# Turning the residual stream's tiles by VectorE blocks and DMA instead of TensorE transposes, in a two-layer decoder trunk

## What is computed

```python
def reference(x, p, g_mix, g_ffn, g_ple, g_final, ...):
    h = x
    for i in range(DEPTH):
        xn = rmsnorm(h, g_mix[i])
        if i % 2 == 0:
            mix = attn_mixer(xn, i, w_in_attn[j], ..., w_out_attn[j])
        else:
            mix = rglru_mixer(xn, w_in_rec[j], ..., w_out_rec[j])
        h = h + mix
        h = h + swiglu(rmsnorm(h, g_ffn[i]), w_ffn_gate[i], w_ffn_up[i], w_ffn_down[i])
        gate = jax.nn.sigmoid(rmsnorm(h, g_ple[i]) @ w_ple_gate[i])
        h = h + gate * (p[i] @ w_ple_proj[i])
    return rmsnorm(h, g_final)
```

## Time and profile before

| | us |
|---|---|
| median of 3 runs | 2414.16 (2414.1 to 2416.4) |
| the profiled execution | 2416.15 |
| its span | 2414.4 |
| VectorE busy | 1333.5 (55%) |
| ScalarE busy | 1128.5 (47%) |
| hardware DMA queue q1, share of 16 engines | 60.2% |
| granted TensorE clock | 0.997 of full |

### The profile page before, as it was taken

One profiled execution on the slowest core, in us unless ns is written; L12 is line 12 of the kernel. 1 busy time (PEld: TensorE's weight loads), 2 busy tenths in 40 slices (PEclk: granted clock), 3 DMA queues, 4 the chain that ended last, 5 costly groups with the idle time before them and its releaser, 6 DMA issues.

```text
span 2414.4 us, 29406 instructions
## 1 busy us (share of the span) xinstructions
PE 2387.1 (99%) x10908; PEld 1974.2 (82%) x10908; DVE 1333.5 (55%) x1655; ACT 1128.5 (47%) x1467; POOL 3.2 (0%) x17
## 2 busy tenths in 40 slices
PE   8999999999999999999999999999999999999997
PEld 7888778888888888888888888888888888888886
DVE  5545666555554555444466677554555555544455
ACT  5425545544444444444454575454444434444454
POOL 0000000000000000000000000000000000000000
PEclk9999999999999999999999999999999999999999
DMA  7744445666766666655557455566766667655563
GB/s 219 235 119 120 123 137 174 182 202 183 226 203 197 216 189 210 202 191 191 191 186 237 146 163 169 191 187 194 218 196 205 212 183 230 201 191 192 191 207 134
DMA packets 250938, 455.42 MB, mean 189 GB/s; under 512 B 21816, under 2 KB 38240, under 8 KB 250720
## 3 DMA queue, kind: packets, MB, share of 16 engines
q1 hardware_dynamic: 250800, 454.18, 60.2%
q10 hardware_dynamic: 48, 0.02, 0.0%
HBM read 440.49 MB, written 2.10 MB: 183 GB/s over the span
## 4 chain that ended last, share of the span: by engine, by line
PE 96%; DVE 1%; ACT 1%; DMA 1%; SPq 0%; issue 0%; ACTq 0%; DVEq 0%
PE ps L1338 30%; PE ps L1340 30%; PE ps L1339 30%; PE ps L1292 1%; PE ps L1549 1%; PE ps L1462 1%; DMA raw<-in_w_in_rec_dram 1%; PE ps L1393 1%; ACT w_hi L571 0%; PE ps L1474 0%; DVE w_lo L816 0%; SPq L494 0%; PE ps L1499 0%; ACT junk L627 0%; PE ps L1500 0%
## 5 line engine op out<-in xcount | busy, mean ns | idle before, releaser
L816 DVE TENSOR_TENSOR w_lo<-raw,w_hi 128x1024 fp32r<-128x1024 f32 x820 | 996.0, 1220 | 996.5 <-ACT w_hi L571 992.4
L571 ACT ACTIVATE w_hi<-raw 128x1024 fp32r<-128x1024 f32 x820 | 859.5, 1054 | 1092.0 <-PE ps L1340 925.1
L1338 PE MATMUL ps<-w_hi,xa_hi 128*128 128x512 f32 x1664 | 647.9, 389 | 0.0
L1340 PE MATMUL ps<-w_hi,xa_lo 128*128 128x512 f32 x1664 | 647.4, 389 | 0.0
L1339 PE MATMUL ps<-w_lo,xa_hi 128*128 128x512 f32 x1664 | 647.3, 389 | 0.0
L1340 PEld LDWEIGHTS ps<-w_hi,xa_lo 128*128 128x128 f32 x1664 | 312.3, 188 | 65.1
L1339 PEld LDWEIGHTS ps<-w_lo,xa_hi 128*128 128x128 f32 x1664 | 312.3, 188 | 64.7
L1338 PEld LDWEIGHTS ps<-w_hi,xa_hi 128*128 128x128 f32 x1664 | 312.3, 188 | 64.4
L1338 PE MATMUL ps<-w_hi,xb_hi 128*128 128x512 f32 x864 | 349.0, 404 | 3.9 <-DVE xb_lo L879 2.3
L1340 PE MATMUL ps<-w_hi,xb_lo 128*128 128x512 f32 x864 | 338.1, 391 | 0.0
L1339 PE MATMUL ps<-w_lo,xb_hi 128*128 128x512 f32 x864 | 337.3, 390 | 0.0
(11 more groups left out here) (201 smaller groups left out, 1022.0 us busy)
## 6 DMA issues: line engine op xcount, KB each, us to landing
raw<-in_w_ffn_gate_dram SPq DMA_DIRECT2D x176, 512.0 KB, 4.5
raw<-in_w_ffn_up_dram SPq DMA_DIRECT2D x176, 512.0 KB, 4.5
raw<-in_w_ffn_down_dram SPq DMA_DIRECT2D x176, 512.0 KB, 4.1
raw<-in_w_in_attn_dram SPq DMA_DIRECT2D x88, 512.0 KB, 3.6
raw<-in_w_ple_gate_dram SPq DMA_DIRECT2D x64, 512.0 KB, 4.3
raw<-in_w_in_rec_dram SPq DMA_DIRECT2D x64, 512.0 KB, 4.1
raw<-in_w_out_attn_dram SPq DMA_DIRECT2D x32, 512.0 KB, 4.3
raw<-in_w_out_rec_dram SPq DMA_DIRECT2D x32, 512.0 KB, 4.0
```

The costliest lines, as they stand in the source:

```text
L571: nc.scalar.activation(w_hi[:, s, 0:n], raw[:, s, 0:n], ACT.Copy).then_inc(hi_ready, 1)
L816: nc.vector.tensor_tensor(w_lo[:, s, 0:n], raw[:, s, 0:n], w_hi[:, s, 0:n].bitcast(F32), ALU.subtract).then_inc(lo_ready, 1)
L1338: nc.tensor.matmul(o, xh[:, k, tok], w_hi[:, s, wk], start=(k == 0), stop=False)
L1340: ins = nc.tensor.matmul(o, xl[:, k, tok], w_hi[:, s, wk], start=False, stop=(k == nkt - 1))
```

## The change

`Kind` gets a flag `move`. It is set for resid, for up, and for ple in layer 0; those kinds have no PSUM banks to turn any more. One path then serves them all:

- VectorE, behind `evacuate` at slot 3: two block transposes, from `stage` for up and from h for the others, into `sg`.
- SyncE: 16 DMAs from `sg` to `stage`, behind the load of slot 7 of the chunk that follows the turned one. Each writes two runs of 128 elements per partition where it wrote one of 256.
- ScalarE, behind the split of slot 6: waits for the 16 DMAs, rounds (one instruction for up, four with a gain for the others).
- VectorE, behind the split of slot 6: the remainders (one or four instructions).
- TensorE: the transposes of h for resid and ple chunks go. In a phase's first chunk it waits for `tiles_ready` instead of `turn_used`.
- ScalarE's sigmoid in ple, which writes `sg`, waits for the moves before it; so does the first gate chunk of an FFN.

```diff
-    resid = Kind("resid", "v", 2, True)
+    resid = Kind("resid", "v", move=True)
...
-        ph.append(Phase(f"ffn{layer}", 11, (8, 8), (Kind("gate", "a"), Kind("up", "v")), "A",
+        ph.append(Phase(f"ffn{layer}", 11, (8, 8), (Kind("gate", "a"), Kind("up", "v", move=True)), "A",
...
-        ple = Kind("ple", "v", 0 if last else 2, True)
+        ple = Kind("ple", "v", move=not last)
...
+            def move_blocks(q, i, r):
+
+                if not q.kinds[r].move:
+                    return
+                sp.wait_ge(blocks_turned, move_no(q, i, r))
                 for a in range(4):
                     for c in range(4):
-                        sp.dma_start(st_blocks[32 * c:32 * c + 32, a], sg_blocks[32 * a:32 * a + 32, c]
-                                     ).then_inc(hid_moved, 16)
+                        sp.dma_start(st_blocks[32 * c:32 * c + 32, :, a],
+                                     sg_blocks[32 * a:32 * a + 32, c].rearrange("p (m x) -> p m x", m=NT)
+                                     ).then_inc(blocks_moved, 16)
...
-                    if (c := hid_chunk(q, i, r, j, 1)) is not None:
-                        move_hid(*c)
+                    if j == 8:
+                        move_blocks(*prev)
+                    if j == 0 and prev and prev[0].slots[prev[2]] == 8 and (two := two_before(q, i, r)):
+                        move_blocks(*two)
                     load_slot(q, i, r, j)
...
+            def round_tiles(q, i, r):
+
+                if not q.kinds[r].move:
+                    return
+                c = column(q, i, r)
+                hi = X[q.dst][0]
+                act.wait_ge(blocks_moved, move_no(q, i, r) * 256)
+                if q.gain is None:
+                    ins = nc.scalar.activation(by_blocks(hi, c), moved_all, ACT.Copy)
+                else:
+                    for k in range(4):
+                        ins = nc.scalar.activation(tile_by_blocks(hi, 4 * c + k), moved_tile(k), ACT.Copy,
+                                                   scale=gain_ap(q.gain, 4 * c + k))
+                ins.then_inc(tiles_hi, 1)
...
                     split_slot(q, i, r, j)
-                    if (c := hid_chunk(q, i, r, j, 1)) is not None:
-                        round_hid(*c)
+                    if j == 6:
+                        round_tiles(*prev)
...
+            def turn_blocks(q, i, r):
+
+                k = q.kinds[r]
+                if not k.move:
+                    return
+                dve.wait_ge(evac["v"], evac_no(q, i, r)[1])
+                c = column(q, i, r)
                 for m in range(NT):
+                    rows = stage[:, m] if k.name == "up" else h[:, m, c * CW:(c + 1) * CW]
+                    dst = sg_blocks.rearrange("p c (m k t) -> p m c k t", k=4, m=NT)[:, m]
+                    ins = nc.vector.transpose(dst, rows.rearrange("p (k c d) -> p c k d", k=4, c=4))
+                ins.then_inc(blocks_turned, 1)
...
                     if j == 3:
                         evacuate(*prev)
-                    if prev[0].kinds[prev[2]].name == "up" and j == 4:
-                        turn_hid(prev[0], prev[1])
-                    if (c := hid_chunk(q, i, r, j, 2)) is not None:
-                        split_hid(*c)
+                        turn_blocks(*prev)
+                    if j == 6:
+                        split_tiles(*prev)
...
-                    elif q.src == "H":
-                        pe.wait_ge(hid_ready, hid_no(q.before, (2 * j + 1) // 4))
+                    elif q.before and q.before.per_move:
+                        pe.wait_ge(tiles_ready, move_no(*maker(q.before, (2 * j + 1) // 4)))
                     else:
                         pe.wait_ge(turn_used, src_turn0(q) + bank_of_ktile(q, j) + 1)
...
-                elif k.name in ("resid", "ple"):
-                    c = 2 * i + r
-                    transpose4(lambda m, f: h[:, m, c * CW + f * P:c * CW + (f + 1) * P], t0)
```

More of the change, by code:

```diff
@@ L64, with __init__ @@
 class Kind:
-    def __init__(self, name, evac, banks=0, split=False):
+    def __init__(self, name, evac, banks=0, split=False, move=False):
         self.name, self.evac, self.banks, self.split = name, evac, banks, split
+        self.move = move
 class Phase:
@@ L123, in build_phases @@
                         stat=6 if last else 3))
-    slot, va, turn, hi = 0, {"v": 0, "a": 0}, 8, 8
+    slot, va, turn, hi, move = 0, {"v": 0, "a": 0}, 8, 8, 0
     for p in ph:
@@ L133, in build_phases @@
         p.per_hi = sum(k.banks for k in p.kinds if k.split)
+        p.move0, p.per_move = move, sum(k.move for k in p.kinds)
+        move += p.per_move * p.pairs
         p.per_v = {e: sum(k.evac == e for k in p.kinds) for e in "va"}
@@ L168, in hi_no, with move_no, maker @@
     return i * p.per_hi + (p.hi0 + sum(k.banks for k in p.kinds[:r] if k.split))
+def move_no(p, i, r):
+    return i * p.per_move + (p.move0 + sum(k.move for k in p.kinds[:r + 1]))
+def maker(p, c):
+    return (p, c, 1) if p.loop else (p, *divmod(c, 2))
 def two_before(p, i, r):
@@ L342, in trunk @@
         turned, turn_hi, turn_used = sem("turned"), sem("turn_hi"), sem("turn_used")
-        hid_turned, hid_rounded, hid_ready = sem("hid_turned"), sem("hid_rounded"), sem("hid_ready")
-        hid_moved = sem("hid_moved")
+        blocks_turned, blocks_moved = sem("blocks_turned"), sem("blocks_moved")
+        tiles_hi, tiles_ready = sem("tiles_hi"), sem("tiles_ready")
         consts, ident_ready, gmix_in = sem("consts"), sem("ident_ready"), sem("gmix_in")
@@ L421, in trunk, with moved_tile, by_blocks, tile_by_blocks @@
         sg_blocks = sg[:].rearrange("p m c -> p (m c)").rearrange("p (c x) -> p c x", c=4)
[L422 to L440, removed]
+        st_blocks = stage[:].rearrange("p m (a x) -> p m a x", a=4)
+        moved_all = st_blocks.rearrange("p m a (k t) -> p (m a) k t", k=4)
+        def moved_tile(k):
+            return moved_all[:, :, k]
+        def by_blocks(t, c):
+            tiles = slice(4 * c, 4 * c + 4) if isinstance(c, int) else bass.ds(4 * c, 4)
+            return t[:, tiles, :].rearrange("p k (b t) -> p b k t", t=32)
+        def tile_by_blocks(t, kt):
+            return t[:, kt].rearrange("p (b t) -> p b t", t=32)
+        def column(q, i, r):
+            return i if q.loop else 2 * i + r
         block = ctx.enter_context(nc.Block())
@@ L457, in load_slot @@
                 sp.dma_start(dst, src).then_inc(raw_in[s], 16)
-            def move_hid(q, i):
-                sp.wait_ge(hid_turned, hid_no(q, i))
+            def move_blocks(q, i, r):
+                if not q.kinds[r].move:
+                    return
+                sp.wait_ge(blocks_turned, move_no(q, i, r))
                 for a in range(4):
                     for c in range(4):
-                        sp.dma_start(st_blocks[32 * c:32 * c + 32, a], sg_blocks[32 * a:32 * a + 32, c]
-                                     ).then_inc(hid_moved, 16)
+                        sp.dma_start(st_blocks[32 * c:32 * c + 32, :, a],
+                                     sg_blocks[32 * a:32 * a + 32, c].rearrange("p (m x) -> p m x", m=NT)
+                                     ).then_inc(blocks_moved, 16)
             def load_vectors():
@@ L585, in evacuate @@
                         if m == 0 and not (isinstance(i, int) and i == 0):
-                            act.wait_ge(hid_moved, hid_no(q, i - 1) * 256)
-                        elif m == 0 and q.name == "ffn1":
-                            act.wait_ge(hid_moved, hid_no(q, -1) * 256)
+                            act.wait_ge(blocks_moved, move_no(q, i - 1, 1) * 256)
+                        elif m == 0:
+                            act.wait_ge(blocks_moved, q.move0 * 256)
                         ins = nc.scalar.activation(sg[:, m], acc, ACT.Silu, scale=rs)
@@ L592, in evacuate @@
                             act.wait_ge(evac["v"], evac_no(q, i, r)[1] - 1)
+                        if m == 0:
+                            act.wait_ge(blocks_moved, 256 * (move_no(q, i, r) - q.kinds[r].move))
                         ins = nc.scalar.activation(sg[:, m], acc, ACT.Sigmoid, scale=rs)
@@ L613, in turn_split @@
                     ins.then_inc(turn_hi, 1)
-            def round_hid(q, i):
-                act.wait_ge(hid_moved, hid_no(q, i) * 256)
-                nc.scalar.activation(by_blocks(X["H"][0], i), sgT, ACT.Copy).then_inc(hid_rounded, 1)
+            def round_tiles(q, i, r):
[11 more added lines that the diff above has]
+                ins.then_inc(tiles_hi, 1)
             def squares(stat, c, wait=None):
@@ L635, in aftermath @@
                 k = q.kinds[r]
[L636 to L639, removed]
+                col = column(q, i, r)
                 if q.stat is not None:
@@ L882, in turn_split, with split_tiles @@
                     ins.then_inc(turn_used, 1)
-            def turn_hid(q, i):
-                dve.wait_ge(evac["v"], evac_no(q, i, 1)[1])
-                for m in range(NT):
```

(24 more changed lines are left out.)

## The result

The changed kernel takes 2539.11 us (median of 4 runs, 2535.46 to 2542.85) against 2414.17 us: 1.0515 times the time before, 95% interval 1.0497 to 1.0533. I had forecast slower and 2493 us with a range up to 2527; the direction holds, the time lies 12 us above the range.

The account below looks back on a forecast made before the run. The prediction took TensorE's queue of work as the bound. New waits of 95.4 us less 16 us of removed transposes made +79 us on the median 2414.16 us, forecast 2493 us, range for 8 in 10 2429 to 2527.

Parts of the forecast that it names:

- The bound, the gain: TensorE's queue bounds the time; removing 160 transposes of h, 20 batches of 0.8 us, gains 16 us.
- The chain: Block transposes, SyncE's 16 issues, landing, rounding, remainders: slot 7's weights come 1.2 us late per FFN chunk, 2.1 per residual chunk.
- the sum: All new TensorE waits over FFN, out, down, ple and first chunks: 95.4 us, less 16, gives +79 us.
- 1.4 us for a late slot 3: Where 8-slot chunks follow each other, slot 3's load waits for slot 7's late remainder, delaying evacuation and chain 1.4 us.
- (a): Moved blocks land as two 512 B rows per partition: issue pitch taken as 0.63 us, ends 0.51 and 0.7.
- (b): VectorE's block transposes with another order of reading and writing: 0.65 us each as now, ends 0.5 and 0.9.
- (c): 320 more DMAs share the rings with the weights; taken at nothing beyond SyncE's time.
- Rival C: Worse: issue pitch 0.7 us or transposes at twice the time; 1.05 us more per chain gives 2537 us; 11%.
- A: Rival: waits stay hidden and the 16 us are gained, 2398 us, if the burst's pitch is 0.42 us; 9%.
- B: Rival: burst pitch about 0.51 us, chains 1.8 us shorter, FFN waits vanish, some 33 us stay: 2431 us; 15%.

Follow-up runs that it names:

- e7: Changed kernel with four of the 16 DMAs replaced by VectorE copies and six of the remaining twelve issued by ScalarE: 2396.64 us, 0.9924 of the kernel before.
- e3: Changed kernel with unused matmuls of constants put ahead of slots whose weights are late, none in out0: 2516.44 us, 1.0413 of the kernel before.
- e5: Changed kernel with the four DMAs that don't change partitions replaced by VectorE copies, twelve DMAs left: 2431.9 us, 1.0068 of the kernel before.
- e6: Changed kernel with twelve DMAs and four VectorE copies, rounding and remainders moved behind slot 7: 2415.63 us, 0.9997 of the kernel before.

## Why the prediction was right and where it failed

- **The bound, the gain.** Right: TensorE's queue was the path, and 160 transposes were 16 us or a little more. e7, where nearly all new waits are gone, is 2415.52 - 2396.64 = 18.9 us faster. In the profiled executions TensorE is idle as long as before (27.6 and 27.3 us) and busy 19.8 us less; 1.7 of that is a stretch at half clock at 358 us that this execution of e7 doesn't have, the rest are the transposes and the 0.09 us behind each batch.
- **The chain.** Right in place, and in size on the whole. SyncE's burst (10.2 us for 10.06), its landing, ScalarE standing still some 7.5 us, slot 7 late: 1.46 us for 1.2 in the FFN, 2.16 (2.00 and the 0.16 of the tail) for 2.1 in down0's first gap, 6.3 for 5.5 and 4.3 and 3.7 for 3.7 in ple0, 3.8 to 5.4 us for 3.6 to 5.2 in the first chunks. Without the gap in xb's second chunk, which isn't the chain's, 96.5 us of gaps and 7 of tails, 103 us, for 95.4. Single terms were off both ways. Down0's second gap is 3.74 us, since the last of its blocks landed 3.6 us after its issue in place of 1.9. The last gaps of out0 and out1 are 1.88 and 1.86 us where the sum has 4.45 and 3.5: its 1.4 us for a late slot 3 isn't there (in out0 that remainder ends at +2.6 us, not at +4.0, perhaps because slot 7 ran at half clock and left the load more time). So the nearness of the total is in part luck.
- **The unknown costs.** (a) was well bounded: two rows of 512 B made the median issue 0.597 us for 0.590. (b) The transposes take 0.69 us alone, as before. (c) I took the extra DMAs at nothing beyond the queue's time. That holds for most bursts; the late landing in down0 (3.6 us) is time that this left out.
- **The step that failed is the sum**: "Together 95.4 us of new waits, less 16". It priced a wait at its own length and left out that the granted clock falls behind it, 32 us here of the 46 by which the forecast was short. e3 shows it apart from the gaps. Idle time of a TensorE that is otherwise never idle cost here (103 + 32)/103 = 1.3 times its length. With this term the same chains give 95.4 + 32 - 16 = 111 on 2414.2, 2526 us. Most of the rest to 2539 is the 8 us by which the chains were short and the 5 us of slower first matmuls.
- **Rival C** had a time as large (2537), but from a slower burst or slower transposes, and neither came. **A and B** fell: the burst didn't get quicker by itself. But their mechanism is what e5 and e7 made true by hand: 2.5 us off the chain took the time from 2539 to 2432. B's price of 2431 was for 1.8 us and without the clock, so that they agree is luck. A's price of 2398 doesn't fit its own condition, which leaves 13 us of waits: that gives 2411. e7 came to 2397 because its blocks land earlier than A supposed.
- **The Trainium skill.** The Trainium skill's figures of about 50 ns a dispatch and little for descriptors (DMA: Bandwidth & Descriptors, Anatomy of one DMA) are told of DMAs that GpSimd issues, and they don't describe SyncE's queue: 672 issues have a median of 0.597 us. The about 2 us fixed a DMA that the Trainium skill gives there agrees with the 1.9 from issue to landing. The Trainium skill also tells, in TensorE: Matmul & The Clock Gate, Part 1, of a gate that passes half of the clock after TensorE has been little busy; the trace agrees, 0.50 behind the gap of 3.74 us. I had not weighed that page, and the forecast has no term for it.

## What to carry to other kernels

A DMA of 32 KB costs its queue about 0.6 us here, more than one of 512 KB (0.37), so a burst of 16 is 10 us in which that queue loads nothing: count issues, not bytes, put them on a second queue whose engine is idle, and copy what needn't cross partitions. In a hand-written order, a wait costs what stands behind it; before moving it, compare when its data lands with when the work behind it is due. And where TensorE is the bound, price a new gap with the clock that it may lose, not with its length alone: in the changed kernel each gap of 3.57 us and more lost it, those of 1.3 us never.

## What I had not expected of the hardware

- A gap of about 2 us costs the clock in some places and not in others: the window over the 2.00 us gap of down0 (1040 to 1060 us) has a granted clock of 1.00, while down1's gap of 2.00 us at 2314.5 is followed by a stretch at 0.50. The gap of 2.31 us ahead of out0, which all the kernels have in the same place, is followed by one in the profiled executions of the kernel before, the changed kernel, e5 and e6, and not in those of the other six.
- Filling the gaps with useless matmuls made the kernel 22.7 us faster (e3).
- ScalarE issuing at the same time doesn't slow SyncE's issues (median 0.599 us in e7, 0.597 alone).
